# A two-layer streaming encoder in fp32 on one core: the first norm's sums on other engines, the first fast unit's sums and its GpSimd work reordered, and the pair work moved behind product 3

## The reference, cut to what matters

```python
def _rms(x, g):
    xf = x.astype(jnp.float32)
    y = xf * lax.rsqrt(jnp.mean(xf * xf, axis=-1, keepdims=True) + EPS) * g.astype(jnp.float32)
    return y.astype(x.dtype)
...
    h = _rms(x, p['norm_mix'])
...
    h2 = _rms(x, p['norm_ffn'])
    gt, up = jnp.split(h2 @ p['w_ffn_in'], 2, axis=-1)
    x = x + (jax.nn.silu(gt) * up) @ p['w_ffn_out']
```

## Time and profile before

| | us |
|---|---|
| median of three runs | 2116.78 |
| the profiled execution, its own time | 2117.41 |
| its span in the profile | 2115.6 |
| TensorE busy (98% of the span) | 2073.4 |
| VectorE busy (73%) | 1536.2 |
| ScalarE busy (55%) | 1161.2 |
| GpSimd busy (25%) | 529.4 |
| DMA, mean rate over the span | 96 GB/s from HBM |

### The profile page before, as it was taken

The page is one execution under the profiler, slowest core; times in us unless marked ns, Lnnn a source line. Parts: engine busy times, 40 slices in busy tenths (PEclk is TensorE's granted clock), DMA queues, the critical chain, the costliest instruction groups (busy, mean ns, idle before and its releaser), DMA issues.

```text
span 2115.6 us, 40337 instructions
## 1 busy us (share of the span) xinstructions
PE 2073.4 (98%) x14418; PEld 1936.3 (92%) x14418; DVE 1536.2 (73%) x3307; ACT 1161.2 (55%) x2565; POOL 529.4 (25%) x415
## 2 busy tenths in 40 slices
PE   8999999999999999999999999999999999999999
PEld 7998868888998999999999987788889989999999
DVE  5467877646848989898645678766477599898984
ACT  4236776566434666566432467665663356566652
POOL 1120030200021554445211200203000234544450
PEclk9999999999999999999999999999999999999999
DMA  5224224233330232222322331341424312222232
GB/s 195 92 85 139 90 79 134 78 94 131 124 120 31 78 103 71 90 76 92 109 99 83 116 117 68 102 139 60 148 78 130 110 44 77 91 75 95 71 105 76
DMA packets 95605, 205.97 MB, mean 97 GB/s; under 512 B 21232, under 2 KB 50544, under 8 KB 95088
## 3 DMA queue, kind: packets, MB, share of 16 engines
q1 hardware_dynamic: 95408, 203.40, 29.5%
HBM read 179.41 MB, written 23.95 MB: 96 GB/s over the span
## 4 chain that ended last, share of the span: by engine, by line
PE 78%; DVE 11%; ACT 4%; DVEq 3%; issue 2%; POOL 1%; DMA 0%; SPq 0%; ACTq 0%
PE ps L1092 15%; PE ps L1018 9%; PE ps L1579 9%; PE ps L1581 9%; PE ps L1580 9%; PE ps L1038 7%; PE ps L1104 5%; DVE op_lo L2764 3%; PE ps L1269 2%; PE ps L1289 2%; PE ps L1165 2%; PE ps L1210 1%; DVEq L2239 1%; PE ps L1383 1%; DVEq L2845 1%
## 5 line engine op out<-in xcount | busy, mean ns | idle before, releaser
L2246 DVE TENSOR_TENSOR w_lo<-raw,w_hi 128x1024 fp32r<-128x1024 f32 (+4 forms) x128 | 146.0, 1141 | 168.3 <-ACT w_hi L1625 163.8
L1092 PE MATMUL ps<-h_hi,w_hi 128*128 128x320 f32 x768 | 246.0, 320 | 0.0
L1092 PE MATMUL ps<-h_hi,w_lo 128*128 128x320 f32 x768 | 237.3, 309 | 0.0
L1092 PE MATMUL ps<-h_lo,w_hi 128*128 128x320 f32 x768 | 237.2, 309 | 0.0
L1625 ACT ACTIVATE w_hi<-raw 128x1024 fp32r<-128x1024 f32 (+4 forms) x128 | 125.8, 983 | 197.2 <-PE ps L1018 115.1
L2199 POOL TENSOR_TENSOR rsq<-ssq,mhalf 128x12 f32<-128x12 f32 (+3 forms) x56 | 117.0, 2090 | 418.8 <-DVE ssq L2358 359.2
L1579 PE MATMUL ps<-th_hi,op_hi 128*128 128x320 f32 x640 | 202.2, 316 | 15.0 <-DVE part L2832 15.0
L2764 DVE TENSOR_TENSOR op_lo<-w_sums,op_hi 128x512 fp32r<-128x512 f32 (+1 forms) x256 | 186.8, 730 | 17.0 <-ACT op_hi L1625 2.6
L1581 PE MATMUL ps<-th_hi,op_lo 128*128 128x320 f32 x640 | 199.1, 311 | 0.0
L1580 PE MATMUL ps<-th_lo,op_hi 128*128 128x320 f32 x640 | 199.0, 311 | 0.0
L1625 ACT ACTIVATE op_hi<-w_sums 128x512 fp32r<-128x512 f32 (+1 forms) x256 | 147.6, 588 | 89.1 <-PE ps L1581 75.7
(11 more groups left out here) (415 smaller groups left out, 6211.2 us busy)
## 6 DMA issues: line engine op xcount, KB each, us to landing
raw<-in_weights SPq DMA_DIRECT2D x176, 512.0 KB, 3.5
raw<-in_weights SPq DMA_DIRECT2D x72, 384.0 KB, 3.0
gates<-gst SPq DMA_DIRECT2D x72, 160.0 KB, 1.8
g<-gates SPq DMA_DIRECT2D x12, 960.0 KB, 6.8
ktb<-in_cache_fox_kt SPq DMA_DIRECT2D x16, 384.0 KB, 4.7
vc<-in_cache_fox_v SPq DMA_DIRECT2D x16, 384.0 KB, 3.7
out_y_t<-x_sb SPq DMA_DIRECT2D x12, 320.0 KB, 2.2
raw<-in_weights SPq DMA_DIRECT2D x8, 416.0 KB, 3.1
```

What stands on the lines that cost most here:

```text
L1092: mm = pe.matmul(ps[:, 5, 0:HALF], w[:, kk * P:(kk + 1) * P], h_pair[x][:, kk, half * HALF:(half + 1) * HALF], start=kk == 0 and n == 0, s ...
L2246: return dve.tensor_tensor(low[:, 0:width], raw[raw_slot(c)][:, 0:width], high[:, 0:width].bitcast(F32), ALU.subtract)
```

## The change

It has three parts. (1) First norm: `first_squares` has a buffer for each of the eight squares, so that ScalarE never waits; VectorE adds part 0's squares, TensorE sums part 1's squares by matmuls against ones (`first_sums`, 24 small matmuls), the table copies stand between VectorE's steps of the norm, the spread of part 1 comes after the fourth block instead of the third, and fewer unread products run. (2) First fast unit: VectorE takes sums 1 and 2 directly behind operand 5, ahead of operand 6; GpSimd's first turn begins when operand 5 is split, not operand 3. (3) The pair work of all pairs stands behind products 3 and 4, as pair 0's did, and GpSimd does its pair parts one turn later, between the third and the fourth sum.

```diff
@@ TensorE, first norm
-                    if first and p:
+                    if first:
                         pe.wait_ge(first_summed.sem, KD - 2)
...
+                def first_sums(steps):
+
+                    for k in steps:
+                        pe.wait_ge(squared.sem, square_at(True, k, 1) + 1)
+                        for n, t in enumerate(PART_TILES[1]):
+                            mm = pe.matmul(ps[:, 3 + n, 0:2], first_squares[:, k, t * P:(t + 1) * P], cst("ones", 0, 2), start=k == 0, stop=k == KD - 1)
+                    if steps[-1] == KD - 1:
+                        mm.then_inc(ln_summed.sem, 1)
...
-                    unread_products(7)
+                    unread_products(2)
                     norm_sum(0, 0)
-                    unread_products(8)
+                    unread_products(4)
                     norm_spread(0, 0)
...
-                        if (p, k) == (0, 0):
+                        if (p, k) in ((0, 0), (0, 1)) and L == 0:
+                            first_sums(range(4 * k, 4 * k + 4))
+                        if (p, k) == (0, 0) and L:
                             norm_sum(0, 1)
-                        if (p, k) == (0, 2):
+                        if (p, k) == (0, 2 if L else 3):
                             norm_spread(0, 1)
@@ ScalarE, squares and pairs
+                        act.activation(first_squares[:, k, PARTS[p]], x_sb[:, k, PARTS[p]], ACT.Square, scale=D ** -0.5).then_inc(squared.sem, 1)
+                        return
...
-                            if m:
-                                for r in range(3):
-                                    pair_high(m, r)
...
-                        if m and 1 <= n <= 4:
-                            pair_high(m, 2 + n)
-                        if m == 0 and n in (3, 4):
+                        if m is not None and n in (3, 4):
                             for r in {3: range(5), 4: (5, 6)}[n]:
                                 pair_high(m, r)
@@ GpSimd
-                    sum_squares(0, 0, [(k, 0) for k in range(1, KD - 1)])
...
-                    c, width, m = fast_chunk(s), fast_width(s), paired(s - 1) if s else None
+                    c, width, m = fast_chunk(s), fast_width(s), paired(s - 2) if s > 1 else None
...
-                    pool.wait_ge(lo_made.sem, lo_made.at(L, made_by(s - 1, 3)))
+                    pool.wait_ge(lo_made.sem, lo_made.at(L, made_by(s - 1, 3 if s > 1 else 5)))
...
                     pool.tensor_tensor(w_sums[:, 2, 0:width], weight_part(s, 0, 0), weight_part(s, 1, 0), ALU.subtract).then_inc(sums_made.sem, 1)
+                    if m is not None:
+                        pair_low(m, 4, 3, pair_first(m))
+                        pair_low(m, 7, 5, ff_act[1][:, 0:HALF])
                     pool.wait_ge(lo_made.sem, lo_made.at(L, made_by(s - 1, 6)))
                     pool.tensor_tensor(w_sums[:, 3, 0:width], weight_part(s, 0, 1), w_sums[:, 1, 0:width], ALU.subtract).then_inc(sums_made.sem, 1)
                     pool.drain()
-                    if m is not None:
-                        pair_low(m, 4, 3, pair_first(m))
-                        pair_low(m, 7, 5, ff_act[1][:, 0:HALF])
@@ VectorE, first norm, first unit, pairs
+                    for k in range(1, KD - 1):
+                        sum_first(k)
                     mean_square(0, 0)
-                    sum_first(1)
+                    table_out(0)
+                    table_out(2)
                     diagonal(0, 0)
...
+                        if k == 5:
+                            mean_square(0, 1)
+                    diagonal(0, 1)
...
                 operand_lo(0, 5)
+                dve.wait_ge(first_out.sem, first_out.at(L, 1))
+                product_sum(0, 1, part[0][:, :], sg[:, 0, second])
+                dve.drain()
+                product_sum(0, 2, part[1][:, :], part[0][:, :])
+                dve.drain()
                 operand_lo(0, 6)
...
-                        if i == 1:
+                        if i == 1 and s:
...
-                        if i == 2 and kind == "in":
+                        if i == 2 and kind == "in" and s:
...
-                        if m and 1 <= pos <= 3:
-                            pair_low(m, pos - 1)
-                            if pos < 3:
-                                pair_total(m, 1 + pos)
-                        if m == 0 and pos == 3:
-                            dve.wait_ge(act_ready.sem, act_ready.at(L, 2))
+                        if m is not None and pos == 3:
+                            if m:
+                                dve.wait_ge(pair_lo_too.sem, pair_lo_too.at(L, 2 * m))
+                            dve.wait_ge(act_ready.sem, act_ready.at(L, 2 * m + 2))
                             pair_total(m, 0)
                             pair_total(m, 1)
                             pair_low(m, 0)
                             pair_total(m, 2)
-                        if m == 0 and pos == 4:
+                        if m is not None and pos == 4:
                             pair_low(m, 1)
                             pair_total(m, 3)
                             pair_low(m, 2)
-                        if m is not None and pos == 4:
                             pair_low(m, 4)
                             pair_low(m, 5)
```

More of the change, by code:

```diff
@@ L998, in norm_sum @@
                         pe.wait_ge(square_summed.sem, square_summed.at(L, 2 * (KD - 2) * q + summed_at(first, KD - 2, p) + 1))
+                    last_squares = first_squares[:, KD - 1, :] if first else squares[:, 1, :]
                     for n, t in enumerate(PART_TILES[p]):
-                        for k, rows in enumerate((square_sum[:, t * P:(t + 1) * P], squares[:, 1, t * P:(t + 1) * P])):
+                        for k, rows in enumerate((square_sum[:, t * P:(t + 1) * P], last_squares[:, t * P:(t + 1) * P])):
                             mm = pe.matmul(ps[:, norm_banks(q, L, p)[0], 2 * n:2 * n + 2], rows, cst("ones", 0, 2), start=k == 0, stop=k == 1)
                     mm.then_inc(ln_summed.sem, 1)
+                def first_sums(steps):
[5 more added lines that the diff above has]
+                        mm.then_inc(ln_summed.sem, 1)
                 def norm_spread(q, p, L=L):
@@ L1656, in square @@
                     if k >= 2:
-                        if first and p:
-                            act.wait_ge(first_summed.sem, max(1, k - 2))
-                        else:
-                            act.wait_ge(square_summed.sem, square_summed.at(layer, 2 * (KD - 2) * q + summed_at(first, max(1, k - 2), p) + 1))
+                        act.wait_ge(square_summed.sem, square_summed.at(layer, 2 * (KD - 2) * q + summed_at(first, max(1, k - 2), p) + 1))
                     act.activation(squares[:, k % 2, PARTS[p]], x_sb[:, k, PARTS[p]], ACT.Square, scale=D ** -0.5).then_inc(squared.sem, 1)
@@ L1683, in _ @@
                         square(0, k, 0)
+                    first_part(0)
                     for k in range(4):
-                        square(0, k, 1)
-                    first_part(0)
-                    for k in range(4, KD):
                         square(0, k, 1)
@@ L2279, in mean_square @@
                     src = ps[:, norm_banks(q, layer, p)[0], 0:2 * len(tiles)].rearrange("p (t e) -> p t e", e=2)[:, :, 0]
+                    if p and q + layer == 0:
+                        src = ps[:, 3:6, 0]
                     dve.tensor_scalar(lnss[:, tiles.start:tiles.stop], src, EPS, None, ALU.add).then_inc(ln_sum.sem, 1)
@@ L2757, in t_lo, with product_sum @@
                     dve.tensor_tensor(th_lo[:, slot, :, :], src, th_hi[:, slot, :, :].bitcast(F32), ALU.subtract).then_inc(th_split.sem, 1)
+                def product_sum(s, i, dst, a):
+                    dve.wait_ge(w_used.sem, w_used.at(L, used_by(s, i)))
+                    return dve.tensor_tensor(dst, a, ps[:, product_bank(s, i), 0:HALF], ALU.add).then_inc(part_made.sem, 1)
                 def operand_lo(s, i):
@@ L2830, in summed @@
                     def summed(dst, a, i):
[L2831 to L2832 removed]
+                        return product_sum(s, i, dst, a)
                     for pos, i in enumerate(ORDERS[s]):
@@ L2836, in _ @@
                             last_low(whole)
-                        if pos == 0 and m:
-                            dve.wait_ge(pair_lo_too.sem, pair_lo_too.at(L, 2 * m))
-                            dve.wait_ge(act_ready.sem, act_ready.at(L, 2 * m + 2))
-                            pair_total(m, 0)
-                            pair_total(m, 1)
-                        if i == 1:
+                        if i == 1 and s:
                             dve.wait_ge(first_out.sem, first_out.at(L, s + 1))
```

44 lines of the change are left out of this document (22 added, 22 removed).

## The result

| | before | changed |
|---|---|---|
| median, us | 2118.11 (2116.57 to 2120.53, 4 runs) | 2158.87 (2156.00 to 2160.68, 4 runs) |
| ratio, 95% interval | | 1.0193 (1.018 to 1.0205) |
| the profiled execution, its own time | 2117.41 | 2160.24 |
| its span | 2115.6 | 2158.5 |

The page of the changed kernel, busy time of each engine. The work is the same as in the earlier trace rows, except for TensorE, whose busy time grew by 14 us: part of what was lost is matmuls that ran slowly, the rest is waits.

A forecast was written before the change was run, and what follows sets the result against it. TensorE was busy 98% of the span, so only its work and waits, mainly for VectorE's `part` sums, could move the time. 2 x (14.8 + 1.8) + 1.7 + 9.6 = +44.5 over 2116.78 gave 2161 us, range 2112 to 2182.

The forecast's parts named there:

- The rule of the port: VectorE operations with two SBUF inputs wait for GpSimd's current operation plus 0.35 us; one gets in between two GpSimd operations.
- Step 1: Pairs 1 to 8, work behind product 3: VectorE's burst meets GpSimd's sums, TensorE waits; +14.8 us a layer.
- Rival A: Pair work: the burst runs free of GpSimd's sums and all waits for pairs go; 2104 us, 16%.
- B: Rival on pair work: VectorE wins the port once more, each of 18 bursts 1.0 us shorter; 2134 us, 15%.
- E: Rival: losses and gains cancel within 4 us, between the free burst and the burst shorter by 1.0; 7%.
- Step 2: First fast unit: the wait moves from product 5 to product 6, pair 0's burst meets GpSimd's sums; +1.8 us a layer.
- Step 3: Start: first product 4 us earlier, 24 small matmuls cost 3.75 more, part 1 starts later; +1.7 us, bounds -2 to +3.3.
- Step 4: Clock: slow matmuls cost 1.6 us behind each of three 2.8 us waits a layer; +9.6 us, bounds 0 and 29.
- Rival C: Clock stays full behind the new waits, everything else as forecast; 2152 us, 18%.
- D: Rival on the clock: it falls after every wait of 1.85 us or more; 2181 us, 7%.

The follow-up runs named there:

- e4: Changed kernel, but in the turn meeting a pair's work GpSimd does its pair parts first, its sums only after operand 5 is split; 2138.82 us, ratio 1.0103.
- e10: e9, plus GpSimd's three sums waiting until operand 5 is split in the turn that meets low parts 4 and 5; 2107.83 us, ratio 0.9947.
- e1: Kernel before with only the change's first norm (part 1 of the change); 2123.97 us against 2116.26, ratio 1.0028.
- e5: Changed kernel with all 24 small matmuls behind the third block instead of 12 behind each of the first two; 2158.70 us, ratio 1.0195.
- e6: Kernel before with the change's first norm, but VectorE adds part 1's squares and six small matmuls remain; 2116.05 us, ratio 0.9995.
- e9: Kernel before with e6's first norm, sum 2 ahead of operand 1 behind pair units, sum 3 ahead of operand 2 in in4, in10, in16; 2108.94 us, ratio 0.9953.
- e7: Kernel before with pairs 0, 1, 3, 4, 6, 7 behind product 3, GpSimd's sums held longer, sums 2 and 3 earlier behind them; 2131.42 us, ratio 1.0066.
- e2: Kernel before with only the pair work moved (part 3 of the change); 2151.38 us, ratio 1.0166.
- e3: Kernel before with only the first fast unit's new order (part 2 of the change); 2115.24 us, ratio 0.9996.

## Why the prediction was right, and where it was not

The time (2161 forecast, 2158.87 measured) and the side are right; but the nearness of the time is luck in part: the sum hides two errors of about 8 and 6.5 us that cancelled.

- **The rule of the port: right, and shown** by e4 and e10. An operation with two SBUF inputs ends 0.35 us after the GpSimd operation under way, and one gets in between two. The Trainium skill (SBUF — State Buffer, Who interferes with whom) calls it an exclusive lock; by that rule the trace agrees (totals of 1.41 and 0.49 us, the same instruction in the same list).
- **Step 1, the pair work: right, in size too.** Sum 6 of in8 was to end 12.2 us after product 3; it ended 12.06 after (821.45, with product 3 of that unit visible at 809.39). Product 3 of in9 waits 1.74 (1.85), product 5 0.51 (0.57), output units 2.64 (2.8); the pair units' own 0.9 is gone. Rival A fell (no burst ran free), and B (total 2 lost the port in all 18 bursts, 1.13 us at least). E fell with them.
- **Step 2, the first unit: right in place, a little high.** Product 6 starts 14.25 us after in2 (14.4) behind a wait of 3.7 (3.8); product 5 of in3 29.6 after (30.2). +1.2 a layer, not +1.8. What it did not say is that a wait now also stands ahead of in3's product 3, and that the slow clock behind product 6 costs 2.9 us where it cost 1.6.
- **Step 3, the start: wrong, the step that failed.** First product 19.39 (19.0), spread to part 1's first product 3.75 (3.86), but the spread at 40.75 instead of 33.9. The failed term is "24 small matmuls ... 3.75 more" with three blocks of 2.1: it took the small matmuls at the duration of six in a stretch of full clock. They took 7.6 us, and the three blocks behind them 3.98, 3.3 and 2.5, the first at half pace and the others partly: 6.1 us more than the forecast's 5.0 and three times 2.1. The upper bound of +3.3 holds the half clock behind the idle stretch, and that came too (1.5 us); it holds nothing for the small matmuls and the blocks. e1, e4 and e5 show the cost with the small matmuls in two places and in one, and a clock that falls with each group at full pace; with six of them (e6) the clock is full from 23.7 on and part 1 starts 2 us earlier than before. The half clock over the first block and the first group was not their doing: it was there before them. Of the +9.9, some 3 us was the luck of one pair of profiles (e1).
- **Step 4, the clock: too high.** I took a fall for each of the six waits of 2.8. It fell behind two of them here, 3.1 us in all in place of 9.6. Rival C (the clock stays full) was nearer for these waits, D (it falls from 1.85 on) is out. The Trainium skill (TensorE: Matmul & The Clock Gate, What's actually happening) ties the half clock to an idle stretch, and says in the same section that the clock goes by how busy TensorE has lately been. The prediction took the first alone; the rows speak against it as the only way down. The clock fell behind two of the six waits, and in e5 it fell while TensorE was busy with small matmuls.

## What to carry to other kernels

Work that a port can hold should not stand in one run: spread out, each stall falls into the waiting engine's idle time; packed, the stalls add up on the chain that the next consumer waits for, above all where the signal that starts the run also releases the other engine. A dozen or more small matmuls in a row cost more than their own time: price the block behind them at half clock too, as it fell with five groups of five here. Six in a row did not bring it down. Put a result that a consumer waits for ahead of an operand that has a unit's time: that move of VectorE's `part` sums, with no work removed, was worth 6 us here by the start times of e9, and what it does has to be read two units on (e7, e9).

## What the runs showed of the hardware that I had not expected

- The same wait has two outcomes. Behind the waits of 2.64 us ahead of product 1 in output units (the changed kernel, e2, e5: 18 of them) the granted clock fell in 8 cases, for 1.5 us each (13.5 in place of 12.0 for the unit), and stayed at 1.00 in 10. Behind the 30 waits of 1.74 in the same traces it never fell; behind six waits of 2.33 in e7 (in6, in12, in18) it fell in five, and behind waits of 3.34 to 3.40 ahead of product 6 of in2 (the changed kernel, e3, e4, e5) in two of five. I did not find what decides.
- The granted clock of the windows view is not to be trusted ahead of its first change: for 19.4 to 32.0 in the changed kernel it says 1.00, while matmuls of 384 columns start 0.32 us apart, as from 35.8 to 39.0 where it says 0.50; at full clock they start 0.17 apart. I went by the pace.
- The 12 small matmuls took 2.6 us at full pace and 5.0 at half, 0.22 and 0.42 each, for two columns.
- One profile of a start is weak evidence: five profiles with the same code up to in2 differ by 5 us there (666.12 to 671.07). The pace of the first row products differs among them too.
